# Products of x with the identity in TensorE's waits of the two routing stages, and three of four tiles' experts chosen ahead

## The reference, cut to what matters

```python
aff = jax.nn.sigmoid((xt @ router_w).astype(jnp.float32))
sel = aff + router_b.astype(jnp.float32)
grp_score = lax.top_k(sel.reshape(-1, N_GROUPS, EXPERTS_PER_GROUP), 2)[0].sum(-1)
_, g_idx = lax.top_k(grp_score, TOPK_GROUPS)            # one group of four experts
...
_, e_idx = lax.top_k(jnp.where(e_mask, sel, -jnp.inf), TOPK_EXPERTS)   # two experts in it
w = jnp.take_along_axis(aff, e_idx, axis=1)
w = w / jnp.sum(w, axis=-1, keepdims=True)
...
for e in range(N_EXPERTS):
    h = jax.nn.silu(xt @ w_gate[e]) * (xt @ w_up[e])
    y = y + gates[:, e:e + 1] * (h @ w_down[e])
```

## Time and profile before

| what | value |
|---|---|
| median of 3 runs (lowest, highest) | 1951.82 (1950.83, 1953.82) |
| the profiled execution: its time, its span | 1950.41, 1948.8 |
| TensorE busy | 1873.6, 96% of the span |
| VectorE, ScalarE, GpSimd busy | 34%, 21%, 5% |
| chain that ended last, by engine | PE 92%, DVE 4%, ACT 2%, issue 1%, DMA 1% |

### The profile page before, as it was taken

One profiled execution on the slowest core, in us unless ns is written; L12 is line 12 of the kernel. 1 busy time (PEld: TensorE's weight loads), 2 busy tenths in 40 slices (PEclk: granted clock), 3 DMA queues, 4 the chain that ended last, 5 costly groups with the idle time before them and its releaser, 6 DMA issues.

```text
span 1948.8 us, 22980 instructions
## 1 busy us (share of the span) xinstructions
PE 1873.6 (96%) x9658; PEld 863.3 (44%) x9658; DVE 653.7 (34%) x1583; ACT 409.9 (21%) x885; POOL 94.0 (5%) x119
## 2 busy tenths in 40 slices
PE   8999999999999999999997999999999996999997
PEld 5444454444444444644544333333644644333332
DVE  5756322223310043114625200003597645100005
ACT  3222021111100003114611111112337601111112
POOL 0001000000000000000000200001001000200001
PEclk9999999999999999999997999999999996999999
DMA  4114812211221121310144699999112133899994
GB/s 171 65 44 152 319 58 86 86 47 72 87 75 65 43 79 45 128 44 1 44 151 157 228 422 415 418 415 331 44 44 98 44 151 140 286 421 416 418 406 180
DMA packets 75416, 336.20 MB, mean 173 GB/s; under 512 B 6776, under 2 KB 18056, under 8 KB 62896
## 3 DMA queue, kind: packets, MB, share of 16 engines
q1 hardware_dynamic: 61056, 285.16, 38.0%
q0 software_dynamic: 11232, 38.30, 5.3%
q10 hardware_dynamic: 3024, 11.25, 1.4%
HBM read 311.07 MB, written 23.09 MB: 171 GB/s over the span
## 4 chain that ended last, share of the span: by engine, by line
PE 92%; DVE 4%; ACT 2%; issue 1%; DMA 1%; ACTq 0%; DVEq 0%
PE psum L634 37%; PE psum L1210 26%; PE psum L948 8%; PE psum L873 4%; PE psum L1086 3%; PE psum L1127 2%; PE psum L1102 2%; PE psum L1029 2%; PE psum L1065 1%; PE psum L1192 1%; PE psum L646 1%; PE psum L1305 1%; PE psum L1236 1%; PE psum L1365 1%; PE psum L754 1%
## 5 line engine op out<-in xcount | busy, mean ns | idle before, releaser
L1210 PE MATMUL psum<-ring,scratch 128*32 128x512 f32 x3840 | 507.9, 598 | 2.9 <-DVE scratch L2405 1.6
L634 PE MATMUL psum<-xT,ring 128*128 128x512 f32 (+1 forms) x1248 | 466.1, 533 | 6.4 <-PE psum L634 4.0
L634 PEld LDWEIGHTS psum<-xT,ring 128*128 128x128 f32 x1248 | 235.1, 190 | 233.9 <-issue 224.4
L1210 PEld LDWEIGHTS psum<-ring,scratch 128*32 128x32 f32 x3840 | 140.4, 111 | 285.3 <-issue 276.8
L634 PE MATMUL psum<-ring,xT 128*128 128x512 f32 (+2 forms) x448 | 168.2, 533 | 0.6 <-PE psum L634 0.6
L948 PE MATMUL psum<-ring,scratch 128*128 128x512 f32 x352 | 152.8, 593 | 1.8 <-PE psum L948 1.5
L1845 DVE SCALAR_TENSOR_TENSOR scratch<-psum,overlay,scratch 128x511 f32<-128x511 f32 x88 | 65.9, 749 | 220.5 <-ACT scratch L1593 219.0
L1210 PE MATMUL psum<-xT,scratch 128*32 128x512 f32 x768 | 127.0, 593 | 0.0
L2403 DVE TENSOR_TENSOR scratch<-psum,scratch 128x512 f32<-128x512 f32 x24 | 16.6, 691 | 310.1 <-PE psum L1210 310.1
L634 PEld LDWEIGHTS psum<-ring,xT 128*128 128x128 f32 x448 | 79.7, 190 | 85.7 <-issue 77.5
L948 PEld LDWEIGHTS psum<-ring,scratch 128*128 128x128 f32 x352 | 66.2, 190 | 87.0 <-issue 87.0
(11 more groups left out here) (389 smaller groups left out, 1672.2 us busy)
## 6 DMA issues: line engine op xcount, KB each, us to landing
ring<-in_moe_w_gate SPq DMA_DIRECT2D x28, 2048.0 KB, 11.0
ring<-in_moe_w_up SPq DMA_DIRECT2D x28, 2048.0 KB, 13.7
ring<-in_moe_w_down SPq DMA_DIRECT2D x24, 2048.0 KB, 12.1
ring<-in_w_up SPq DMA_DIRECT2D x11, 2048.0 KB, 9.1
xT<-in_moe_w_down SPq DMA_DIRECT2D x8, 2048.0 KB, 11.8
expert_rows<-scratch ACTq DMA_DIRECT2D x20, 512.0 KB, 10.9
ring<-in_w_down SPq DMA_DIRECT2D x4, 2048.0 KB, 8.2
ring<-in_even_w_in SPq DMA_DIRECT2D x4, 2048.0 KB, 7.8
```

The source lines that it names most:

```text
L634: mm = nc.tensor.matmul(out_, lhsT, rhs, start=(j == 0), stop=(j == len(pairs) - 1))
L1210: mm = nc.tensor.matmul(bank[r, :], lhsT[:, t, r], w_[:, t, c0:c0 + 512], start=(t == 0), stop=(t == nk - 1))
```

## The change

Two things change in both layers. First, TensorE gets products whose result nobody reads: the stationary operand is the identity, the moving one is 256 columns of x, the target is banks[2]. Six stand ahead of the wait for the choice, six ahead of the wait for the tables, nine ahead of the wait for the gathered rows. Second, the choice is made in two parts: the logits of tile 3 go to banks[6] instead of banks[4], ScalarE takes a Sigmoid of tiles 0 to 2 between the copies of tile 2 and tile 3 and a second one of tile 3, and VectorE runs the whole series of choosing instructions twice, once for three tiles, once for one, with the sums over earlier tiles between them.

```diff
+        EARLY = NT - 1
+        def logits(n):
+            return banks[4][:, n * E:(n + 1) * E] if n < EARLY else banks[6][:, 0:E]
...
-                product(banks[4][:, n * E:(n + 1) * E],
+                product(logits(n),
                         [(xT[:, t, n * P:(n + 1) * P], router_w[:, t, :]) for t in range(KD)]).then_inc(routed, 1)
...
+            def keep_busy(times):
+
+                for _ in range(times):
+                    nc.tensor.matmul(banks[2][:, 0:256], ident, x[:, 0, 0:256], start=True, stop=True)
+
             def route(l):
 
                 flat = lambda a: a.rearrange("p a b -> p (a b)")
+                keep_busy(6)
                 pe.wait_ge(chosen_ready, l + 1)
                 nc.tensor.matmul(banks[7][:, 0:5 * E], operand["before"], flat(chosen5), start=True, stop=False)
                 pe.wait_ge(earlier_ready, l + 1)
...
                     .then_inc(ranks_mm, 1)
+                keep_busy(6)
                 for j in range(2):
                     pe.wait_ge(hot_ready, 2 * l + j + 1)
...
                 mm.then_inc(idx_mm, 1)
+                keep_busy(9)
...
-                if stage in ("even_out", "odd_out"):
-
-                    act.wait_ge(routed, NT if stage == "even_out" else 2 * NT)
-                    A(aff.rearrange("p a b -> p (a b)"), banks[4][:, 0:NT * E], ACT.Sigmoid).then_inc(aff_ready, 1)
+                    if stage in ("even_out", "odd_out") and n - late in (EARLY - 1, NT - 1):
+                        a, b = (0, EARLY) if n - late < EARLY else (EARLY, NT)
+                        act.wait_ge(routed, b if stage == "even_out" else NT + b)
+                        A(aff[:, a:b, :].rearrange("p a b -> p (a b)"), banks[4][:, 0:EARLY * E] if a == 0 else logits(a), ACT.Sigmoid)\
+                            .then_inc(aff_ready, 1)
...
+            def choose(l, a, b):
+                m = b - a
+                t, t4, t8, t16 = (slice(k * a, k * b) for k in (1, 4, 8, E))
+                dve.wait_ge(aff_ready, 2 * l + (1 if a == 0 else 2))
+                step(V.tensor_tensor(sel[:, t], aff[:, t], operand["router_b"].unsqueeze(1).to_broadcast(wide), ALU.add))
...
             def route(l):
                 V.memset(chosen5[:, NT, :], 0.0)
+                choose(l, 0, EARLY)
+                step(V.tensor_tensor(chosen[:, 0:EARLY], hot[:, 0, 0:EARLY], hot[:, 1, 0:EARLY], ALU.add))
                 V.tensor_copy(earlier[:, 0, :], chosen[:, 0, :])
                 step(V.tensor_tensor(earlier[:, 1, :], chosen[:, 0, :], chosen[:, 1, :], ALU.add))
                 step(V.tensor_tensor(earlier[:, 2, :], earlier[:, 1, :], chosen[:, 2, :], ALU.add))
+                choose(l, EARLY, NT)
+                V.tensor_tensor(chosen[:, EARLY:NT], hot[:, 0, EARLY:NT], hot[:, 1, EARLY:NT], ALU.add).then_inc(chosen_ready, 1)
+                dve.wait_ge(chosen_ready, l + 1)
                 V.tensor_tensor(earlier[:, 3, :], earlier[:, 2, :], chosen[:, 3, :], ALU.add).then_inc(earlier_ready, 1)
```

More of the change, by code:

```diff
@@ L2284, in _ @@
             flat = lambda a: a.rearrange("p a b -> p (a b)")
+            def choose(l, a, b):
+                m = b - a
+                t, t4, t8, t16 = (slice(k * a, k * b) for k in (1, 4, 8, E))
+                wide = [P, m, E]
+                groups = lambda v: v[:, t4].rearrange("p (n g) -> p n g", g=4)
+                by_group = lambda v: v[:, t].rearrange("p n (g i) -> p (n g) i", i=4)
+                line = lambda v: v.rearrange("p a b -> p (a b)")
+                dve.wait_ge(aff_ready, 2 * l + (1 if a == 0 else 2))
+                step(V.tensor_tensor(sel[:, t], aff[:, t], operand["router_b"].unsqueeze(1).to_broadcast(wide), ALU.add))
+                two = sel[:, t].rearrange("p n (h i) -> p (n h) i", i=2)
+                V.tensor_tensor(hi[:, t8], two[:, :, 0], two[:, :, 1], ALU.max)
+                step(V.tensor_tensor(lo[:, t8], two[:, :, 0], two[:, :, 1], ALU.min))
+                hi2, lo2 = (v[:, t8].rearrange("p (g i) -> p g i", i=2) for v in (hi, lo))
+                V.tensor_tensor(top1[:, t4], hi2[:, :, 0], hi2[:, :, 1], ALU.max)
+                V.tensor_tensor(top2[:, t4], hi2[:, :, 0], hi2[:, :, 1], ALU.min)
+                step(V.tensor_tensor(gsum[:, t4], lo2[:, :, 0], lo2[:, :, 1], ALU.max))
+                step(V.tensor_tensor(top2[:, t4], top2[:, t4], gsum[:, t4], ALU.max))
+                step(V.tensor_tensor(gsum[:, t4], top1[:, t4], top2[:, t4], ALU.add))
+                step(V.tensor_reduce(best[:, t], groups(gsum), AX.X, ALU.max))
+                step(V.tensor_tensor(groups(gpick), groups(gsum), best[:, t].unsqueeze(2).to_broadcast([P, m, 4]), ALU.is_equal))
+                step(V.scalar_tensor_tensor(gpick[:, t4], gpick[:, t4], -8.0, operand["group_of"][:, t4], ALU.mult, ALU.add))
+                step(V.tensor_reduce(lowest[:, t], groups(gpick), AX.X, ALU.min))
+                step(V.tensor_tensor(groups(gpick), groups(gpick), lowest[:, t].unsqueeze(2).to_broadcast([P, m, 4]), ALU.is_gt))
+                step(V.scalar_tensor_tensor(by_group(masked), gpick[:, t4].unsqueeze(2).to_broadcast([P, m * 4, 4]), NEG,
+                                            by_group(sel), ALU.mult, ALU.add))
+                for j in range(2):
+                    step(V.tensor_reduce(best[:, t], masked[:, t], AX.X, ALU.max))
+                    step(V.tensor_tensor(tmp16[:, t], masked[:, t], best[:, t].unsqueeze(2).to_broadcast(wide), ALU.is_equal))
+                    step(V.scalar_tensor_tensor(line(tmp16[:, t]), line(tmp16[:, t]), -32.0, operand["expert_of"][:, t16], ALU.mult, ALU.add))
+                    step(V.tensor_reduce(lowest[:, t], tmp16[:, t], AX.X, ALU.min))
+                    step(V.tensor_tensor(hot[:, j, t], tmp16[:, t], lowest[:, t].unsqueeze(2).to_broadcast(wide), ALU.is_equal))
+                    V.tensor_scalar(first_place[:, j, t], lowest[:, t], float(CAP), float(32 * CAP), ALU.mult, ALU.add)
+                    if j == 0:
+                        step(V.scalar_tensor_tensor(line(masked[:, t]), line(hot[:, 0, t]), 2 * NEG, line(masked[:, t]), ALU.mult, ALU.add))
@@ L2286, in route @@
             def route(l):
[L2287 to L2290, removed]
                 V.memset(chosen5[:, NT, :], 0.0)
-                two = sel.rearrange("p n (h i) -> p (n h) i", i=2)
-                V.tensor_tensor(hi, two[:, :, 0], two[:, :, 1], ALU.max)
-                step(V.tensor_tensor(lo, two[:, :, 0], two[:, :, 1], ALU.min))
@@ L2297, in route @@
[L2297 to L2321, removed]
@@ L2322, in route @@
-                V.tensor_tensor(chosen, hot[:, 0], hot[:, 1], ALU.add).then_inc(chosen_ready, 1)
-                dve.wait_ge(chosen_ready, l + 1)
+                choose(l, 0, EARLY)
+                step(V.tensor_tensor(chosen[:, 0:EARLY], hot[:, 0, 0:EARLY], hot[:, 1, 0:EARLY], ALU.add))
                 V.tensor_copy(earlier[:, 0, :], chosen[:, 0, :])
```

## The result

The changed kernel takes 1940.91 us (median of 6 runs, 1937.05 to 1943.19) against 1952.74 before (6 runs, 1950.83 to 1956.08): ratio 0.9938, 95% interval 0.9928 to 0.9948, about 12 us less. Its profiled execution took 1939.79 and has a span of 1938.1, 10.7 less than before.

A forecast was written before the change was run, and what follows sets the result against it. TensorE, busy 96% of the span, was taken as the bound, with time won in its routing waits and half-clock work. Terms of 5.25 and 6.73 us, together 12.0, cut to 11.0, gave 1940.8; range 1938.0 to 1946.5.

The forecast's parts named there:

- the choice: VectorE's choosing series for tile 3 alone has narrower steps: 0.65 us less a layer, between nothing and 0.8.
- L1174 and L1177 to VectorE's start: Small TensorE work behind the choice runs at full clock: 1.40 us becomes 0.72, 0.68 less a layer.
- L1182 to the list: TensorE's 12-column products ahead of the list run at full clock: 3.58 us becomes 1.85, 1.73 less a layer.
- list to first transpose (gather, third batch): Nine products in the 4.81 us wait for gathered rows take 3.98 at full clock, so cost nothing.
- transposes and copies: Preparing the first group's rows, 2.67 us from first transpose to first product, runs at full clock: 0.78 less a layer.
- first group of experts: Its 128 records take 13.87 us at full clock instead of 15.28 and 16.76: 1.41 and 2.89 less.
- The first batch: Six products before the choice, at most 5.31 us, hidden by VectorE's work; clock rises within or right behind.
- Rival 1: Clock falls again before the experts, under small work or transposes: only 7.7 us less, 1944.1; chance 0.13.
- the allowance: About 1 us taken off the 12.0 sum for a late clock rise in one of the two layers, giving 11.0.
- The prediction's own sign of being wrong: Wrong if the clock is at 0.50 in either later batch, or the first group of experts still starts slow.
- Rival 3: Products never raise the clock; second and third batches delay by 2.38 and 3.16 us a layer: 1961.6; chance 0.04.
- The rule that transposes do not count: Transposes before the experts count as idle for the clock, which may drop again, leaving 7.7 us less.

The follow-up runs named there:

- 6, 0, 0: Changed kernel with only the six products ahead of the wait for the choice, the second and third calls left out: ratio 0.9982.
- the four further products: Changed kernel plus four products a layer: two between routing tiles 1 and 2, one before tile 3's, one amid the 12-column products: 1943.13, ratio 0.9952.
- both kinds of transposes: Changed kernel with 128x128 transposes replacing the products, in two versions: 22, 12 and 20 (ratio 0.9939), and 22, 22 and 34 (ratio 0.9933).
- narrow products: Changed kernel with identity products of 16 columns instead of 256, 24, 13 and 21 in the three places: 1971.71, ratio 1.0097.
- 22, 22, 34 transposes: Changed kernel with 128x128 transposes in place of the products, 22, 22 and 34 in the three places: ratio 0.9933.
- 22, 12, 20 transposes: Changed kernel with 128x128 transposes in place of the products, 22, 12 and 20 in the three places: 1941.27, ratio 0.9939.
- products alone: Kernel before with the three batches of six, six and nine products added, the choice left in one part: 1944.77, ratio 0.9955.

## Why the prediction was right

The time was forecast at 1940.8 and is 1940.91. The mechanism is the one forecast: the clock rose in the first batch of both layers, the small work behind it ran at full clock, and the experts began at full clock. That the two figures agree to 0.1 is luck: the six runs spread over 6 us, and the kernel before, too, has a median of 1952.74 over six runs where the forecast started from 1951.82.

The terms, from the two timelines of each layer (expected, then measured in the first and the second); they add up to the 5.44 and 6.16 by which the lengths fell:

| term | expected | first | second |
|---|---|---|---|
| end of tile 3's routing to L1187 (the choice) | 0.65 | 0.85 | 0.86 |
| L1174 and L1177 to VectorE's start | 0.68 | 0.75 | 0.73 |
| L1182 to the list | 1.73 | 1.63 | 1.64 |
| list to first transpose (gather, third batch) | 0 | 0.10 | -0.78 |
| transposes and copies | 0.78 | 0.78 | 0.89 |
| first group of experts | 1.41 and 2.89 | 1.34 | 2.82 |

- *The choice* was sized low. VectorE's series itself is 0.88 shorter in the first layer. The steps with 64 elements do shrink by 0.05, but those with 16 before have 4 now and shrink a little too, 0.195 from start to start in place of 0.205, which the prediction had left out; the steps from L2310 on, where most of the wide ones stand, are 0.66 of the 0.88. The first three tiles' series lay beside tile 3's work as forecast, ended at 1053.66, and VectorE then waited 0.38 us for the Sigmoid; I had worked out 0.1 to spare. (The range counts the choice's upper bound, 0.15, once, where two layers make it 0.3; its lower end would be 1937.9.)
- *The first batch* cost nothing and the clock rose in it, after 4.0 and 4.7 us. The other traces show 2.7 to 6.0 from the start of their first batch, and in four of their layers it rose only behind it (the first with 6, 0, 0 and with the four further products, the second with both kinds of transposes).
- *Rival 1*, a fall under small work, did take place, in the second layer, but behind L1196 and not ahead of the experts; priced at 1.41 and 2.89 it cost 0.78, since the third batch was long enough to restore the clock. I had taken about 1 us off the full sum for one mishap in one layer, for a late rise; the mishap was this one, so that the allowance had the right size is luck.
- *The prediction's own sign of being wrong* did appear. It was to be wrong "if the clock is at 0.50 in either of the two later batches", and in the second layer it was, for 3.4 of the third batch's 5.82 us. What does not hold there is that the clock, once up, stays up until the experts have begun. The sum survived it, since a batch that starts warm and ends warm overruns its wait by far less than the 3.16 priced for one at half clock throughout.
- *Rival 3's prices*, full payment for what exceeds a wait, are borne out by the doubled batches, whose second and third, 5.40 and 8.02 long, cost 2.0 and 2.9 where 2.38 and 3.16 stood. What did not come is its condition, a clock that stays down. The narrow products show that condition, with batches still longer, at ratio 1.0097.
- *The rule that transposes do not count.* The prediction set a rule of the Trainium skill ("TensorE: Matmul & The Clock Gate", Part 4: PE-mode transpose) beside the rows and went by the rows. The runs with transposes settle it for float32 here: 22 transposes behind 16-column products brought the granted clock to 1.00, and with filled waits the ratio is 0.9933. The measurement decides against what the Trainium skill says there.
- *Where the traces' randomness enters.* In the first layer, behind the same instructions, the clock fell anywhere from 4.3 us (with narrow products, with seven in the third place) to 7.6 us (22, 22, 34 transposes) after the first transpose of tile 1. The rise differs as much: in the kernels that start with the same six products it came 2.8 to 6.0 us into them. The Trainium skill ("TensorE: Matmul & The Clock Gate", Part 1: The HAM clock gate) says of the rise that its point differs by some 500 ns from run to run; the traces agree that it differs, and show more. This moves single terms by 1 to 2 us in a run, which may be much of the 6 us between the fastest and the slowest run of the changed kernel; that is argued and not shown, since one execution of each kernel has a trace.

What stays open: why the clock falls where L1196 ends or up to 0.8 behind it in some executions (second layer of the changed kernel, both layers with 22, 22, 34 transposes, first layer with seven in the third place) and not in others (first layer of the changed kernel, both layers with doubled batches), under the same instructions of this stretch. The product inserted in the middle did not prevent it in the second layer of that kernel. Nor is it shown what a fall needs: small work, a pause and the work ahead of both change together in these kernels.

## What to carry to other kernels

Where a chain of small steps on other engines leaves TensorE waiting a few microseconds at a time, look at the granted clock and not at the busy share: the waits themselves may be unavoidable, but the half speed of the steps between them and of the heavy work behind need not be. In this kernel it paid to fill the waits with wide work whose length at full clock is just under the wait, and to fill all of them in a row: the first batch alone was worth 0.0006 of the time, the third alone 0.0017, all three 0.0050. Size each against its wait, since nearly all that exceeds it is paid: twice the work gave everything back.

## What the runs showed of the hardware that was not expected

- The granted clock rose from 0.50 to 1.00 under 128x128 float32 transposes as it did under products with 256 columns: 2.7 and 4.2 us into a batch of 22 in the first layers, right behind it, 5.1 us after its start, in the second layers.
- A TensorE busy 1.00 is no sign of a rising clock: it stayed at 0.50 through 28.9 us without a gap, 24.4 of them 16-column products.
- The clock fell 1.1 us into a wait of 2.93 us (6, 0, 0, second layer), and at the end of one of 2.10 us behind a batch (products alone, first layer). Behind shorter pauses it mostly held (1.65 and 1.62 us in the first layer with 22, 12, 20 transposes), but not always: with the products alone, in the second layer, a fall came 1.0 us behind a pause of 1.59. It also fell where no pause since the first batch had been over 0.4 us: in the changed kernel's second layer, 0.4 behind the end of the 12-column products and 0.6 into a batch of wide ones.
